# Up matmuls of a decoder layer that walk their 512 columns in blocks of 16, in the order 0, 8, 16, 24, 1, 9 and so on

## The reference

```python
def peer(x, w_query, sub_keys_1, sub_keys_2, expert_down, expert_up):
...
    top_s, pos = lax.top_k(cand_s, PEER_TOPK)
    expert_idx = jnp.take_along_axis(cand_i, pos, axis=-1)
    gates = jax.nn.softmax(top_s, axis=-1)
...
    def chunk(args):
        xt, et, gt = args
        u = expert_down[et]
        h = jax.nn.gelu(jnp.einsum('cd,ced->ce', xt, u), approximate=False)
        vv = expert_up[et]
        return jnp.einsum('ce,ced->cd', gt * h, vv)
```

## Time and profile before

| | us |
|---|---|
| median of 3 runs | 2432.74 |
| lowest, highest | 2431.49, 2433.75 |
| the profiled execution | 2433.66 |
| its span | 2431.4 |
| TensorE busy in the span | 2404.8 (99%) |
| VectorE, ScalarE, GpSimd busy | 1569.1, 1197.4, 594.7 |
| moved by the DMA engines | 539.01 MB, mean 222 GB/s |
| granted TensorE clock, mean | 0.998 |

### The profile page before, as it was taken

How to read it: one execution, slowest core, us unless ns; L and a number is a source line. 1 busy time by engine, 2 the same in 40 slices (tenths; PEclk the granted TensorE clock), 3 DMA queues, 4 the chain that set the end, 5 groups by cost and what they waited for, 6 DMA issues and landing times.

```text
span 2431.4 us, 45146 instructions
## 1 busy us (share of the span) xinstructions
PE 2404.8 (99%) x15884; PEld 2207.9 (91%) x15884; DVE 1569.1 (65%) x2615; ACT 1197.4 (49%) x1787; POOL 594.7 (24%) x427
## 2 busy tenths in 40 slices
PE   8999999999999999999999999999999999999997
PEld 8999999999999999999999999999888888888886
DVE  5555555546666666888888887755655555555556
ACT  4444444545444444666555655454444444444444
POOL 0000000000000000477668886786000000000000
PEclk9999999999999999999999999999999999999999
DMA  7667666554445665588888998988776777677764
GB/s 270 217 217 223 220 227 210 179 190 151 157 141 172 192 197 184 192 222 220 227 288 223 255 276 288 281 225 259 241 240 230 240 242 242 232 239 242 243 233 139
DMA packets 182918, 539.01 MB, mean 222 GB/s; under 512 B 53664, under 2 KB 53664, under 8 KB 180432
## 3 DMA queue, kind: packets, MB, share of 16 engines
q1 hardware_dynamic: 124128, 449.89, 56.3%
q0 software_dynamic: 54128, 71.68, 12.0%
q10 hardware_dynamic: 4608, 16.78, 2.2%
HBM read 501.42 MB, written 35.78 MB: 221 GB/s over the span
## 4 chain that ended last, share of the span: by engine, by line
PE 98%; DVE 1%; DMA 1%; ACT 0%; issue 0%; DVEq 0%; ACTq 0%; SPq 0%
PE ps L1256 38%; PE ps L1477 28%; PE ps L1452 17%; PE ps L1453 9%; PE ps L1456 1%; PE ps L1295 1%; PE ps L1310 1%; PE ps L1455 1%; PE ps L1303 0%; PE ps L1297 0%; DMA raw<-stream 0%; PE ps L1430 0%; PE ps L1311 0%; PE ps L1290 0%; DVE u_s L1209 0%; DVE u_s L1219 0%
## 5 line engine op out<-in xcount | busy, mean ns | idle before, releaser
L756 DVE TENSOR_TENSOR w_first<-raw,w_first 128x1024 fp32r<-128x1024 f32 x425 | 521.0, 1226 | 367.0 <-ACT w_first L457 355.9
L390 POOL DMA_INDIRECT g_dram<-lists x256 | 442.7, 1729 | 97.8 <-issue 79.1
L457 ACT ACTIVATE w_first<-raw 128x1024 fp32r<-128x1024 f32 x425 | 447.8, 1054 | 4.2 <-DMA raw<-stream 3.3
L756 DVE TENSOR_TENSOR w_second<-raw,w_second 128x1024 fp32r<-128x1024 f32 x299 | 365.9, 1224 | 5.4 <-ACT w_second L457 5.0
L1452 PE MATMUL ps<-a_all,w_first 128*128 128x480 f32 x1024 | 345.8, 384 | 0.2 <-DVE w_first L756 0.2
L1256 PE MATMUL ps<-a_all,w_first 128*128 128x256 f32 x2520 | 315.0, 281 | 9.2 <-DVE w_first L756 9.2
L457 ACT ACTIVATE w_second<-raw 128x1024 fp32r<-128x1024 f32 x299 | 314.6, 1052 | 7.2 <-DMA raw<-stream 6.3
L1256 PEld LDWEIGHTS ps<-a_all,w_first 128*128 128x128 f32 x2520 | 299.2, 189 | 10.2 <-issue 9.2
L1256 PE MATMUL ps<-a_all,w_second 128*128 128x256 f32 x2520 | 303.9, 276 | 0.0
L1452 PE MATMUL ps<-a_all,w_second 128*128 128x480 f32 x896 | 302.1, 382 | 0.0
L1256 PEld LDWEIGHTS ps<-a_all,w_second 128*128 128x128 f32 x2520 | 294.4, 188 | 0.0
(11 more groups left out here) (230 smaller groups left out, 3410.2 us busy)
## 6 DMA issues: line engine op xcount, KB each, us to landing
raw<-stream SPq DMA_DIRECT2D x850, 512.0 KB
g_dram<-blank POOLq DMA_DIRECT2D x32, 512.0 KB, 6.2
a_dram<-act ACTq DMA_DIRECT2D x32, 512.0 KB
a_in<-a_dram POOLq DMA_DIRECT2D x32, 512.0 KB, 5.0
g_in<-g_dram POOLq DMA_DIRECT2D x32, 512.0 KB, 6.5
g_dram<-lists POOLq DMA_INDIRECT x256
res<-x_t SPq DMA_DIRECT2D x4, 512.0 KB, 7.0
ln_s<-ln POOLq DMA_DIRECT2D x1, 2048.0 KB, 7.4
```

The lines of the kernel that those rows point to most:

```text
L390: pool.indirect_dma_start(out=g_cell, out_offset=bass.IndirectOffsetOnAxis(ap=lists[0:n, tt, 1, j, c:c + 1], axis=0), in_=lists[0:n, tt, 2 ...
L457: act.activation(weights(t, hf, moved)[0], raw[:, t.slot(hf), :], ACT.Copy).then_inc(hi_ready, 1)
L756: dve.tensor_tensor(low, raw[:, s, :], high.bitcast(F32), ALU.subtract).then_inc(lo_ready, 1)
```

## The change

The matmul of up gets its output and its moving operand through a function turned, which cuts the 512 columns as (a b c) with a = 4, b = 8, c = 16 and has them walked with b outermost, then a, then c: 16 words in a row, then the 16 that lie 128 words further on, four times, and then back to the second block. The blocks so come in the order 0, 8, 16, 24, 1, 9, 17, 25 and so on to 31. Output and moving operand have the same order, so that each column's product lands in its place. The stationary operand, up_bank and all other matmuls are left as they are.

```diff
--- before.py
+++ after.py
@@ -1246,6 +1246,10 @@
     def _(pe):
         pe.sem_inc(half_used, HALVES_FREE)
 
+        def turned(v, n):
+
+            return v.rearrange("p (a b c) -> p b a c", a=n, c=16)
+
         def half_ready(t, hf):
             pe.wait_ge(lo_ready, t.half(hf) + 1 + HALVES_FREE)
 
@@ -1474,7 +1478,7 @@
                     for q, (m, w) in enumerate(((m_hi, high), (m_hi, low), (m_lo, high))):
                         for c in range(2):
                             o = D * tt + HALF * hf + 512 * c
-                            ins = pe.matmul(ps[:, o:o + 512], m[:, b % 2, s], w[:, 512 * c:512 * c + 512],
+                            ins = pe.matmul(turned(ps[:, o:o + 512], 4), m[:, b % 2, s], turned(w[:, 512 * c:512 * c + 512], 4),
                                             start=first and q == 0, stop=False, skip_group_check=True)
                 ins.then_inc(half_used, 1)
 
```

## The result

The changed kernel takes 2454.11 us (median of 4 runs, 2453.59 to 2454.79); the kernel before, run beside it, 2432.32. The ratio is 1.0089, with a 95% interval of 1.0072 to 1.0107: slower by 21.8 us. The forecast was 2412, in a range from 2388 to 2440.

A forecast was written before the change was run, and what follows sets the result against it. The prediction took TensorE's train of up matmuls, by its start-to-start gap, to bound the kernel. Saving 21.0 us on the moving read and 0 for breaks took 2433.66 to 2412.7, about 2412 against the median; range 2388 to 2440.

The forecast's parts named there:

- Where the time is: Up stage, line 1477: TensorE always busy, so only the 228.9 ns gap between matmul starts counts, 15.6 ns above streaming.
- The floor: Up matmuls: 215 ns a gap is reachable, taken from fp32 matmuls of 256 columns, leaving 13.9 ns avoidable.
- Term 1: Moving read in the up stage: the new order saves half the avoidable excess, 6.95 ns a matmul, 21.0 us in all.
- One meeting per load: Up stage, plain order: the moving read gains a lap on each weight load; the new order gives half a meeting on average.
- The eight places: SBUF reads: assumed that a meeting costs when moving read and weight load are in the same of eight 64-byte places.
- Term 2: Up matmuls: the new pattern's 31 breaks in read and PSUM write, taken to cost 0.
- far bound: Worst case for the breaks: the trace's slowest streaming, first tile, 219 ns per 256 columns, so 438 ns for 512.
- The reading of the 256-column chains: Two fp32r chains, 113.3 and 117.9 ns gaps: the excess depends on how streams fall against each other.
- The 3 ns of w_second: Up halves read from w_second, 128 bytes further on: the moving operand's address moves the gap by 3 ns.
- C: Rival for line 1477: jumps in the moving read or PSUM write make it slower, put at 2592 us; chance 0.20.
- lower price: Line 1477: one column time (0.42 ns) a break with the predicted gain kept, +18 us, 2451 us.

The follow-up runs named there:

- fp32_orders: The kernel before with both up operands read as fp32 and a different column order in each half tile; up stage 4385.84 us in all.
- read_only: The changed kernel with the PSUM write put back in plain order, only the moving read reordered; 2455.25 us, gap 236.67 ns.
- places8: Stationary operands of the loop's eight tiles at eight 64-byte offsets, halves in plain or changed order; plain gaps 226.7, 233.3, 232.9, 228.9 ns, repeating modulo 256 bytes.
- places4: Stationary operands at four 64-byte offsets, each with four other column orders instead of plain and changed; gaps 233.3 to 242.5 ns.
- one_place: Stationary operands stored with a step of 64 words, so each load stays in one 64-byte place, with several read orders; reported gaps 239.9 to 246.2 ns.
- load_width: Up matmuls' stationary operand cut to 64 or 32 of 128 columns in some tiles, various orders; plain gaps 229.0, 228.4, 231.1 ns at widths 128, 64, 32.
- cols256: Up matmuls cut into twice as many of 256 columns, each half tile with its own order; plain gaps 113.3 ns in one half, 117.8 and 117.9 in two.
- shift_plain: The kernel before, plain order, with the stationary operands moved 16 words further on; 2424.79 us beside 2431.17, ratio 0.9972.

## Why the prediction was wrong

- **Where the time is.** Right: one line, one stage, no wait anywhere, the gap alone decides, the instructions of all other stages untouched, and VectorE and ScalarE with slack. The change of gap times 3023 is the whole change of the stage.
- **The floor.** "So 215 is a floor that this trace does reach": wrong for fp32r. It came from fp32 rows. The x2 in the row of line 1310 is one matmul of the code, which so takes 0.43 us and not half of it, and fp32_orders shows that such a matmul streams each column for longer and loses nothing in any order with runs of four columns or more. No fp32r order, place or width in these runs settled below 226.7 ns for 512 columns, or 113.3 for 256. Of the 13.9 ns that I called avoidable, 2.2 were, and not by the order.
- **Term 1, which failed.** "One meeting per load ... half a meeting on average. So half of the excess: 6.95 ns". The new order doesn't halve the excess of 15.6 ns, it raises it to 23.3. read_only shows all of the rise in the moving read: 236.67 ns, +7.8 for the -6.95 of the term. The eight places are four (places8), and the price isn't one meeting for each lap (places4, one_place). What the loss does depend on is the length of the runs in the moving read: over 512 columns nothing from 256 bytes on, below that 4 to 15 ns at runs of 32 to 128 bytes. The change went from one run of 2048 bytes to 32 of 64 bytes. The reading behind the term, that the moving read and the weight read get in each other's way, isn't refuted as a whole: the distance between their addresses moves the plain gap from 226.7 to 233.3 ns, and with short loads 4x16 loses nothing against plain (load_width). What failed is the count of meetings that turned it into a gain.
- **Term 2.** Right for the write, 0 at any number of jumps. Wrong for the read, but not as a price per jump either: 7.8 / 31 = 0.25 ns here, 0.07 for 4x8, 0.36 for 2x16, 0 for 2x64. Its far bound was misread: all but the first two of the 24 matmuls of the earlier trace rows start 213 to 214 ns apart, one column in a cycle of 1.2 GHz, and from the 27th on 118 ns apart. TensorE had been idle until then, at 9.22 us. So this fits the lower of the two clock levels, though the row of that stretch shows a granted clock of 1.00, and isn't a price of streaming. The forecast doesn't use it.
- **The reading of the 256-column chains.** Their two gaps were taken as a matter of where streams lie. cols256 has both values in the plain order with both operands at the same places modulo 256 bytes; the halves differ in what ran just before, and in which of the two slots they read. The 3 ns of w_second are a matter of address, as I took them: its 128 bytes are two of the four places.
- **The rivals.** C had the sign and the place, and its lower price, one column time a jump, gave 2451. That this is near 2454 is luck: it adds a gain that isn't there to a price per jump that isn't one. I put the case at 2592 instead and cut the range at 2440, below both; that end left out exactly the small loss that my own arithmetic had named.

What stays open is why runs below 256 bytes cost at the fp32r rate, and what the load has to do with it. Its address moves the gap by up to 6.7 ns, and its length takes away the loss of 4x16 but of no other order that was tried. Most gaps settle in whole multiples of 16 cycles over one to three matmuls (7 in three before, 7 in two after), which looks like a waiting in fixed steps, but no run shows the thing that is waited for.

## What to carry to other kernels

Where TensorE never waits, measure the gap from start to start to a tenth of a nanosecond and change one side of one operand at a time: the read, the write, the start address. At the fp32r rate let the moving read walk at least 256 bytes in a row; how PSUM is written made no difference in any order tried here, all of which keep pairs of columns together. And a floor taken from another data type is no floor.

## What the runs showed that I had not expected

- The gap depends on where the stationary operand begins modulo 256 bytes, and not modulo 512: 226.67, 233.33, 233.3 and 228.89 ns for four places in steps of 64 bytes. Sixteen words of padding made the whole kernel faster by 0.28% (0.17 to 0.39).
- Several orders lock onto one value from very different conditions: 2x16 has 240.0 ns (576 = 512 + 64 cycles) at all four places, with loads of 108 to 188 ns, and 120.0 over 256 columns.
- A chain of equal matmuls can run in one of two rhythms. The down stage has 5.293 us a tile throughout in the kernel before and 5.280 in the changed one, with the same instructions and addresses; shift_plain goes over from the first to the second after about a third of the stage, and load_width from the second to the first. For 256 columns it is 113.3 or 117.8 ns, 4% apart. So a stage that an edit doesn't touch can differ by some 2 us here. What chooses the rhythm was not tried.
